# The second block's gates: five steps a layer stand inside runs of small products

## The chip, the core and the metric

The kernel runs on one core of a Trainium2 chip. The metric is the device time of one execution in microseconds, as the median of several runs. The engines are TensorE (PE for its products, PEld for its weight loads), VectorE (DVE), ScalarE (ACT), GpSimd (POOL) and SyncE (SP, which issues most of the DMAs).

## The reference, cut to what matters

Two blocks of different architecture run over 256 tokens of width 1024, each with two layers, all in float32. The first block (gated mixing, attention, cross attention, experts) isn't touched. A layer of the second block computes:

```python
p = n @ w_in                                    # columns for the recurrence, for latent attention, and the gates
p_r, p_k, p_v, p_w, p_a, p_g = split(token_shift(p_rw))
gate_a, gate_b = split(p[..., SHIFT_COLS + MLA_COLS:], 2)      # 2 x 1024 columns
y_a = _rwkv7_time_mix(p_r, p_k, ...) @ w_out_rwkv              # the recurrence
y_b = _mla(q_lat, kv_lat, k_pe, ...) @ w_out_mla               # attention over latents
merged = sigmoid(gate_a) * y_a + sigmoid(gate_b) * y_b
h = h + merged @ w_out
h = h + _conv_ffn(rmsnorm(h), w_ffn_up, conv_w, conv_b, w_ffn_down)
```

The recurrence is, per head of 64 columns (8 heads) and per token, `state = state * w + (state @ a) b + v k`, `y = state @ r`.

## The kernel before

**The recurrence in chunks.** `tensor_rwkv` (TensorE), `vector_rwkv` and `scalar_rwkv` work on the 256 tokens in 8 chunks of 32 (`CH`, `NCH`), for 4 pairs of heads (`PAIRS`) and 2 tiles of 128 tokens (`NT`), so 16 units (`UNITS`). The products inside a chunk are small, 32x32 to 64x64. `chunks` makes, in 64 products, one 32x32 matrix per unit and chunk (L2220); `blocks` multiplies such matrices to invert a triangle (L2238); `wide` makes 128x128 ones (L2230); `turn` transposes (L2210). Then come the rows u (L2314), W and U (L2325), the outputs (L2334), the inner products for the chunks' ends (L2345, first for G, 48 products, then for H, 112), and last the states, one chunk after the other (L2386, L2390), each of which waits for VectorE (L3156). A float32 product is issued as two products and two weight loads, so 64 of the program's are 128 products and 128 loads in the trace.

**The gates between them.** The 2048 gate columns are 4 quarters j of 512, for 2 token tiles t, with 8 slices k of the inner width 1024: 64 steps. A step is one slice of one output tile [128 tokens x 512]. For j = 0 and 1 it is one float32 product (L2191), for j = 2 and 3 it is `exact`: three products of split high and low parts (L578), each with its weight load. These steps depend on nothing in the recurrence; they fill TensorE while ScalarE and VectorE work on the small products' results. `fill(point)` issues the steps of one point of the table `GATE_FILLS`; the order of the steps is fixed (`gate_step`), the table only says how many stand at which point. The points behind step 44 were before:

- "close", steps 45 to 47: ahead of `chunks(4, kt, a0)`, the keys' run of L2220
- "rows", 48 to 52: behind it and eight transposes, ahead of the u products (L2314)
- "wu", 53 to 55: ahead of L2325; "q", 56 and 57: ahead of the outputs; "g", 58: behind the G products
- "h", 59 to 62: behind the H products, while VectorE makes H (L3148); "rest", 63: behind the states

The outputs of t = 0 and 1 sit in PSUM banks 6 and 7. When a tile's eighth slice is done, ScalarE takes the sigmoid out of the bank (`gate_rows` in `scalar_rwkv`, L2764), and the next tile's first step of that bank waits for it (`gates_sig`). For j = 3, the tiles' first four slices are steps 48 to 51 and 52 to 55, the last four 56 to 59 and 60 to 63; step 47 ends a tile of j = 2. ScalarE's stream has its `gate_rows` at fixed points, each taking the tiles that the table says are done there (`gates_done`). The first product of step 48 signals that the weights of j = 2 are no longer read (L2199); SyncE waits for that and loads the next 2 MB into this slot of the ring.

**Who issues what.** There is no scheduler: each engine's instructions stand in the order of the code, and every wait is a semaphore's. An own wait instruction (L2174) shows where a product waits for more than one.

Of the kernel before, what the change touches and what calls it, by code (L numbers as in the profile page):

```python
# [47 lines left out]
PAIRS = RW // P  # L48
# [492 lines left out]
def slab(m, slot, k, n):  # L541

    return m.ring[:, slot, 0:k * n].rearrange("p (k n) -> p k n", n=n)
# [1582 lines left out]
def _gate_fills():  # L2126
    at = 0
    for point, n in (("open", 8), ("prep", 5), ("sums", 3), ("masks", 2), ("second", 3), ("second_wide", 3), ("fourth", 3),
                     ("whole", 2), ("fourth_wide", 3), ("eighth", 2), ("keys", 4), ("block", 3), ("block_wide", 2), ("cross", 2),
                     ("close", 3), ("rows", 5), ("wu", 3), ("q", 2), ("g", 1), ("h", 4)):  # L2130
        GATE_FILLS[point] = (at, at + n)
        at += n
    GATE_FILLS["rest"] = (at, 2 * PAIRS * KD)


_gate_fills()
EXACT_GATES = 2


def gate_step(i):  # L2140

    j, r = i // (2 * KD), i % (2 * KD)
    if j < EXACT_GATES:
        return j, r // KD, r % KD
    return j, r // 4 % 2, r // KD * 4 + r % 4
# [7 lines left out]
def gate_rows_split(m):  # L2153

    room = m.ring_lo[:, PLAN2[W_GATES].slot]
    return room[:, 0:SLAB // 2], room[:, SLAB // 2:], m.hT[:, :, :].rearrange("p k n -> p (k n)")
# [10 lines left out]
def tensor_rwkv(m, pe, l, landed, used):  # L2167
# [3 lines left out]
    tiles = [(p, t) for p in range(PAIRS) for t in range(NT)]  # L2171

    def wait(signal, k=None):
        pe.wait_ge(*at(signal, l, k))  # L2174

    def fill(point):

        for i in range(*GATE_FILLS[point]):
            j, t, k = gate_step(i)
            n = 2 * j + t  # L2180
            out, tokens = ps[:, 6 + t, :], slice(t * P, (t + 1) * P)
            if k == 0:
                if n < 2:
                    wait("kk_root")
                else:
                    wait("gates_sig", n - 1)
            if j < EXACT_GATES:
                if k == 0 and t == 0:
                    landed(W_GATES + j)
                w = slab(m, PLAN2[W_GATES + j].slot, KD, BANK)  # L2190
                ins = mm(out, m.hT[:, k, tokens], w[:, k, :], start=k == 0, stop=k == KD - 1)  # L2191
            else:
                if k % 4 == 0 and t == 0:
                    wait("gate_lo", 2 * (j - EXACT_GATES) + k // 4 + 2)
                rows = [a.rearrange("p (k n) -> p k n", n=T)[:, k, tokens] for a in gate_rows_split(m)[:2]]
                w = [a.rearrange("p (k n) -> p k n", n=BANK)[:, k % 4, :] for a in gate_half(m, j, k // 4)[:2]]
                first, ins = exact(m, out, rows, w, k == 0, k == KD - 1)
                if j == PAIRS - 1 and k == 0 and t == 0:
                    first.then_inc(used(W_GATES + j - 1), 1)  # L2199
            if k == KD - 1:  # L2200
                ins.then_inc(s("gates_full"), 1)
            elif j == EXACT_GATES and t == 1 and k == 3:
                ins.then_inc(s("gates_half"), 1)
# [6 lines left out]
                ins = nc.tensor.transpose(ps[:, b, c0:c0 + P], src[:, 2 * half + i, t * P:(t + 1) * P], m.ident)  # L2210
        ins.then_inc(s("tok_T"), 1)

    def chunks(b, lhs, rhs):

        for i, (p, t) in enumerate(tiles):
            for c in range(CT):
                tokens = slice(t * P + c * CH, t * P + (c + 1) * CH)
                for h in range(2):
                    r = slice(h * HD, (h + 1) * HD)
                    ins = mm(ps[c * CH:(c + 1) * CH, b + h, i * CH:(i + 1) * CH], lhs[r, p, tokens], rhs[r, p, tokens],  # L2220
                             start=True, stop=True)
        ins.then_inc(s("prod_full"), 1)
# [18 lines left out]
    def unit(p, t, h):  # L2241
        return h * PAIRS * NT + p * NT + t

    a0, bt, kt, rr = m.KK, m.A, m.LW, m.C
# [56 lines left out]
    blocks(2, M["D"], M["D2T"])  # L2301
    fill("close")
    wait("prod_masked", 8)
    chunks(4, kt, a0)
    for half in range(2):
        turn((0, 3)[half], a0, half)
    fill("rows")
    wait("prod_masked", 9)
    wait("tok_a", 2)
    for h in range(2):  # L2310
        for i, (p, t) in enumerate(tiles):
            for c in range(CT):
                r = slice(c * CH, (c + 1) * CH)
                ins = mm(ps[r, 4 + h, i * HD:(i + 1) * HD], M["Aak"][r, unit(p, t, h), :],  # L2314
                         m.vtok[r, p, t * P + h * HD:t * P + (h + 1) * HD], start=True, stop=True)
        ins.then_inc(s("u_full"), 1)
# [30 lines left out]
    def head(a, p, t, h):  # L2347
        return a[:, p, t * P + h * HD:t * P + (h + 1) * HD]
# [11 lines left out]
        outputs(g, lambda p, t, h: head(m.vtok, p, t, h), m.Ark, lambda p, t: False, False)  # L2360
    wait("g_set")
    for p, t in tiles:
        for part in range(2):
            for c in range(CT):
                if t * CT + c < NCH - 1:
                    for h in range(2):
                        u1 = m.WU[:, unit(p, t, h), HD:]
                        lhs, rhs = ((head(m.btok, p, t, h), u1), (head(m.ktok, p, t, h), head(m.vtok, p, t, h)))[part]
                        ins = inner(p, t, c, h, lhs, rhs, part == 0, part == 1)
# [984 lines left out]
```

## Time and profile before

| | us |
|---|---|
| median of 3 runs | 2261.44 |
| lowest, highest | 2258.86, 2265.96 |
| the profiled execution | 2257.99 |
| its span, first to last instruction | 2256.2 |
| mean granted TensorE clock | 0.930 of full speed |

The times of single instructions come from the profiled execution. The second block begins at about 1330 us; its layers' recurrences with the gates lie at 1407 to 1517 us and at 1857 to 1966 us. In the rows, "issue" in the chain of waits is time in which TensorE had no instruction under way and waited for nothing that the profile shows. L578 is the line of `exact`, L2345 that of the inner products for G and H.

### The profile page before, as it was taken

The page shows a single profiled execution, that of the slowest core. Times are in us where ns is not written, and L with a number is a line of the kernel's source. Part 1 is how long each engine was busy: PE and PEld are TensorE (multiplying, and loading weights), DVE is VectorE, ACT ScalarE, POOL GpSimd, SP SyncE. Part 2 cuts the span into 40 slices and gives each one's busy share as a digit, 9 for nine tenths or more (in the row PEclk, how much of TensorE's full clock was granted, in tenths as well). Part 3 has the DMA queues.
Part 4 walks back from the last instruction along what each step waited for, and adds up shares of the span by engine and source line. Part 5 has one row for each costly group of instructions (what it writes and reads, how often), then busy time and mean ns, then how long its engine had stood idle before and what let it go on. Part 6 is the DMA issues. An engine that isn't in the chain of part 4 may idle for free.

```text
span 2256.2 us, 38410 instructions
## 1 busy us (share of the span) xinstructions
PE 2035.7 (90%) x17052; PEld 1392.2 (62%) x17052; DVE 894.9 (40%) x1280; ACT 718.2 (32%) x1015; POOL 40.8 (2%) x65
## 2 busy tenths in 40 slices
PE   8999988887779999987787789999999999999998
PEld 6887433333327887432333339675899796758996
DVE  6444211100106444111111117546677475476774
ACT  5444111111105453111111125314444453144442
POOL 1000000000001000000000000000000000000000
PEclk9999888888889998888888889999999999999999
DMA  8246899999996257899999996023754360237540
GB/s 324 85 141 274 365 428 428 428 428 429 429 423 249 75 187 308 360 428 428 429 429 428 428 412 238 4 71 119 235 187 169 107 227 4 76 113 226 187 178 19
DMA packets 139667, 592.33 MB, mean 263 GB/s; under 512 B 5744, under 2 KB 59200, under 8 KB 114448
## 3 DMA queue, kind: packets, MB, share of 16 engines
q1 hardware_dynamic: 138432, 586.67, 65.5%
q0 software_dynamic: 1104, 3.70, 0.4%
q8 instruction: 109, 1.79, 0.3%
q14 instruction: 22, 0.18, 0.0%
HBM read 589.30 MB, written 1.05 MB: 262 GB/s over the span
## 4 chain that ended last, share of the span: by engine, by line
PE 69%; DMA 24%; DVE 3%; ACT 2%; issue 2%; SPq 1%; DVEq 0%; POOLq 0%; ACTq 0%; POOL 0%
PE ps L578 36%; DMA ring<-in_w_up 22%; PE ps L1182 11%; PE ps L2191 3%; PE ps L2006 2%; PE ps L904 2%; DMA ring<-in_w_in 1%; PE ps L1144 1%; PE ps L2238 1%; PE ps L1205 1%; PE ps L1214 1%; PE ps L595 1%; PE ps L1003 1%; PE ps L1099 1%; PE ps L1079 1%
## 5 line engine op out<-in xcount | busy, mean ns | idle before, releaser
L1182 PE MATMUL ps<-ring,area 128*32 128x512 f32 x1920 | 308.5, 716 | 122.1 <-DMA ring<-in_w_up 122.1
L554 DVE TENSOR_TENSOR ring_lo<-ring,slab_hi 128x2048 fp32r<-128x2048 f32 x136 | 311.3, 2291 | 226.7 <-ACT slab_hi L549 226.4
L549 ACT ACTIVATE slab_hi<-ring 128x2048 fp32r<-128x2048 f32 x136 | 260.0, 1913 | 288.1 <-PE ps L578 266.9
L1182 PEld LDWEIGHTS ps<-ring,area 128*32 128x32 f32 x1920 | 72.6, 128 | 312.6 <-issue 159.4
L578 PE MATMUL ps<-hT_hi,slab_hi 128*128 128x256 f32 x832 | 234.7, 282 | 3.0 <-DVE hT_lo L571 1.6
L578 PE MATMUL ps<-hT_lo,slab_hi 128*128 128x256 f32 x832 | 233.4, 280 | 0.0
L578 PE MATMUL ps<-hT_hi,ring_lo 128*128 128x256 f32 x832 | 232.5, 279 | 0.0
L1771 DVE TENSOR_TENSOR area<-ps,par 128x256 f32<-128x256 f32 x32 | 13.6, 425 | 484.9 <-PE ps L1144 484.9
L1421 ACT ACTIVATE area<-ps 128x512 f32<-128x512 f32 x32 | 19.1, 597 | 539.8 <-PE ps L1182 539.8
L1205 PE MATMUL ps<-ring,area 128*32 128x512 f32 x992 | 158.6, 795 | 32.3 <-DVE area L1791 29.8
L578 PEld LDWEIGHTS ps<-hT_hi,slab_hi 128*128 128x128 f32 x832 | 156.0, 188 | 4.2 <-issue 2.2
L578 PEld LDWEIGHTS ps<-hT_hi,ring_lo 128*128 128x128 f32 x832 | 158.0, 190 | 0.0
L578 PEld LDWEIGHTS ps<-hT_lo,slab_hi 128*128 128x128 f32 x832 | 156.3, 188 | 0.0
L1144 PEld LDWEIGHTS ps<-area,xn 128*128 128x128 f32 x1024 | 124.4, 202 | 27.1 <-issue 27.1
L578 PE MATMUL ps<-slab_hi,hT_hi 128*128 128x512 f32 (+1 forms) x320 | 125.2, 391 | 6.1 <-DVE hT_lo L571 4.1
L1144 PE MATMUL ps<-area,xn 128*128 128x32 f32 x1024 | 128.0, 286 | 1.8 <-DVE area L1755 1.8
L578 PE MATMUL ps<-ring_lo,hT_hi 128*128 128x512 f32 (+1 forms) x320 | 123.9, 387 | 0.0
L578 PE MATMUL ps<-slab_hi,hT_lo 128*128 128x512 f32 (+1 forms) x320 | 122.9, 384 | 0.0
L1214 PE MATMUL ps<-area 128*128 128x512 f32 x256 | 118.4, 605 | 0.0
L1205 PEld LDWEIGHTS ps<-ring,area 128*32 128x32 f32 x992 | 36.3, 140 | 131.6 <-issue 90.3
L1214 PEld LDWEIGHTS ps<-area 128*128 128x128 f32 x256 | 46.0, 189 | 73.0 <-issue 45.9
L1793 DVE COPY area<-ps 128x512 f32<-128x512 f32 x32 | 22.1, 691 | 168.6 <-PE ps L1205 168.6
(384 smaller groups left out, 3159.0 us busy)
## 6 DMA issues: line engine op xcount, KB each, us to landing
ring<-in_w_up SPq DMA_DIRECT2D x62, 2048.0 KB, 20.4
ring<-in_w_down SPq DMA_DIRECT2D x62, 2048.0 KB, 21.6
ring<-in_w_gate SPq DMA_DIRECT2D x56, 2048.0 KB, 15.2
ring<-in_w_ffn_up SPq DMA_DIRECT2D x44, 1024.0 KB, 7.7
ring<-in_w_in SPq DMA_DIRECT2D x18, 2048.0 KB, 10.1
ring<-in_w_ffn_down SPq DMA_DIRECT2D x10, 2048.0 KB, 7.8
ring<-in_xattn_w_kv SPq DMA_DIRECT2D x8, 2048.0 KB, 16.8
area<-in_w_gate SPq DMA_DIRECT2D x6, 2048.0 KB, 13.9
```

The source lines that it names most:

```text
L549: return m.nc.scalar.activation(hi, whole, ACT.Copy)
L554: return m.nc.vector.tensor_tensor(lo, whole, hi, ALU.subtract)
L578: ins = m.nc.tensor.matmul(out, lhs[a], rhs[b], start=start and i == 0, stop=stop and i == 2)
L595: ins = m.nc.tensor.transpose(m.ps[:, b, k * T + t * P:k * T + (t + 1) * P], src[:, t, cols(2 * b + k)], m.ident)
L904: ins = mm(out, w[:, k, c * P:(c + 1) * P], rhs[:, k, :], start=k == 0, stop=k == KD - 1)
L1003: ins = mm(ps[:, score_bank(t), h * HD:(h + 1) * HD], m.pT[:, j, kt, :], m.raw[:, kt, c:c + HD], start=kt == 0, stop=kt == 1)
L1144: ins = mm(ps[:, 2, k * CAP:(k + 1) * CAP], m.xn[:, t, k * P:(k + 1) * P], m.onehot[:, t, :], start=t == 0, stop=t == NT - 1)
L1182: ins = mm(ps[32 * g:32 * g + CAP, 1, :], m.tokT[:, k, :], gate_up[i][:, k % 4, (g % 2) * BANK:(g % 2 + 1) * BANK], start=k == 0, stop=k = ...
L1205: ins = mm(ps[32 * c:32 * c + CAP, 2 + nh, :], m.hid[:, c, half, :], down[half][:, c, nh * BANK:(nh + 1) * BANK], start=half == 0, stop=ha ...
L1214: ins = mm(ps[:, 4 + 2 * nh + t, :], m.pick[:, t * P:(t + 1) * P], m.dn[:, nh, :], start=False, stop=True, skip_group_check=True)
L2006: ins = mm(ps[:, 4 * j + i, :], src[:, k, t * P:(t + 1) * P], w[:, k, nh * BANK:(nh + 1) * BANK], start=k == 0, stop=k == 3)
L2191: ins = mm(out, m.hT[:, k, tokens], w[:, k, :], start=k == 0, stop=k == KD - 1)
```

## The change

The table has three new points, and `fill` is called in the midst of three runs of small products: "keys_in" after half of the keys' run, "u_in" between the two halves of the u products, "h_in" between the pairs 0, 1 and the pairs 2, 3 of the H products. The steps keep their order, so the counts of the points between shift: "close" has 45 and 46, "keys_in" 47, "rows" 48 to 50, "u_in" 51 and 52, "wu" 53 and 54, "q" 55 and 56, "g" 57, "h_in" 58 and 59, "h" 60 to 63, and "rest" none.

```diff
@@ -2127,7 +2127,7 @@
-                     ("close", 3), ("rows", 5), ("wu", 3), ("q", 2), ("g", 1), ("h", 4)):
+                     ("close", 2), ("keys_in", 1), ("rows", 3), ("u_in", 2), ("wu", 2), ("q", 2), ("g", 1), ("h_in", 2), ("h", 4)):
@@ -2210,9 +2210,11 @@
-    def chunks(b, lhs, rhs):
+    def chunks(b, lhs, rhs, within=None):
 
         for i, (p, t) in enumerate(tiles):
+            if within and i == len(tiles) // 2:
+                fill(within)
@@ -2301,13 +2303,15 @@
-    chunks(4, kt, a0)
+    chunks(4, kt, a0, "keys_in")
@@ -2301,13 +2303,15 @@
     for h in range(2):
+        if h:
+            fill("u_in")
         for i, (p, t) in enumerate(tiles):
@@ -2360,6 +2364,8 @@
     wait("g_set")
     for p, t in tiles:
+        if p == PAIRS // 2 and t == 0:
+            fill("h_in")
         for part in range(2):
```

The order of TensorE's instructions around the keys' run and the u products, before; ps is PSUM, ring_lo the low parts of the weights, area the recurrence's matrices, x3 of L578 are one step:

```order
L578 MATMUL ps<-ring_lo 128x512 x9
L2220 MATMUL ps<-area 32x32 [waits prod_masked]
L2220 MATMUL ps<-area 32x32 x63
L2210 MATMUL ps<-con,area 128x128 x8
L578 MATMUL ps<-ring_lo 128x512 [waits gate_lo,gates_sig]
L578 MATMUL ps<-ring_lo 128x512 x11
L578 MATMUL ps<-ring_lo 128x512 [waits gates_sig]
L578 MATMUL ps<-ring_lo 128x512 x2
L2314 MATMUL ps<-area,ring 32x64 [waits tok_a,prod_masked]
L2314 MATMUL ps<-area,ring 32x64 x63
L578 MATMUL ps<-ring_lo 128x512 x9
```

And now (the lines have moved by two and four):

```order
L578 MATMUL ps<-ring_lo 128x512 x6
L2222 MATMUL ps<-area 32x32 [waits prod_masked]
L2222 MATMUL ps<-area 32x32 x31
L578 MATMUL ps<-ring_lo 128x512 x3
L2222 MATMUL ps<-area 32x32 x32
L2210 MATMUL ps<-con,area 128x128 x8
L578 MATMUL ps<-ring_lo 128x512 [waits gate_lo,gates_sig]
L578 MATMUL ps<-ring_lo 128x512 x8
L2318 MATMUL ps<-area,ring 32x64 [waits tok_a,prod_masked]
L2318 MATMUL ps<-area,ring 32x64 x31
L578 MATMUL ps<-ring_lo 128x512 x3
L578 MATMUL ps<-ring_lo 128x512 [waits gates_sig]
```

One step has moved from ahead of the keys' run into it, and two from ahead of the u products into them; the wait of step 52 for ScalarE's sigmoid now stands within the u products.

In the H products on TensorE, the place between pair 1 and pair 2 now reads as follows; before, no L578 stood between the rows of L2345:

```order
L2349 MATMUL ps<-xn,area 64x64 x6
L2349 MATMUL ps<-area 64x64 x6
L578 MATMUL ps<-gate_hi,ring_lo 128x512
L578 MATMUL ps<-ring_lo 128x512
L578 MATMUL ps<-gate_hi,ring_lo 128x512 x2
L578 MATMUL ps<-ring_lo 128x512
L578 MATMUL ps<-gate_hi,ring_lo 128x512
L2349 MATMUL ps<-xn,area 64x64 x8
L2349 MATMUL ps<-area 64x64 x8
```

Two steps, 58 and 59, stand behind 56 of the 112 H products. On ScalarE one sigmoid of the gates (L2764, now L2770), that of the tile which step 47 ends, has moved from ahead of the four copies of the turned keys to behind them, as its stream shows now:

```order
L549 ACTIVATE gate_hi<-ring 128x2048 [waits gates_half]
L2770 ACTIVATE ring<-ps,stat 128x512 [waits gates_full]
L2816 ACTIVATE area<-ps 128x4x64 [waits tok_T]
L2816 ACTIVATE area<-ps 128x4x64
L2816 ACTIVATE area<-ps 128x4x64 [waits tok_T]
L2816 ACTIVATE area<-ps 128x4x64
L2770 ACTIVATE ring<-ps,stat 128x512 [waits gates_full]
L2821 ACTIVATE area<-ps 128x8x64 [waits u_full] x2
```

Before, both sigmoids stood ahead of the copies (L2764 x2). VectorE's, GpSimd's and SyncE's instructions keep their order.

## Rows read from the trace of the kernel before

**Rows 1.** Page, parts 1 and 4: busy time of TensorE; the chain by engine

```profile
PE 2035.7 (90%) x17052; PEld 1392.2 (62%) x17052; DVE 894.9 (40%) x1280; ACT 718.2 (32%) x1015; POOL 40.8 (2%) x65
...
PE 69%; DMA 24%; DVE 3%; ACT 2%; issue 2%; SPq 1%; DVEq 0%; POOLq 0%; ACTq 0%; POOL 0%
```

**Rows 2.** Chain that ended last, layer 1: start us, us, what

```profile
1455.11 2.78 PE ps L578 x12
...
1470.39 2.27 PE ps L578 x9
1472.66 1.22 PE ps L2220 x78
...
1474.90 3.44 PE ps L578 x15
1478.34 1.90 PE ps L2314 x122
1480.24 2.62 issue
...
1483.16 3.63 PE ps L578 x9
...
1501.79 1.51 issue
...
1504.16 4.54 PE ps L578 x12
```

**Rows 3.** The same chain, layer 2

```profile
1922.82 1.36 PE ps L2220 x81
...
1931.33 1.86 issue
...
1952.20 1.55 issue
```

**Rows 4.** Windows from block border to block border (first row: the columns)

```profile
core 0: us, PE busy (x) PEld busy (x) DVE busy (x) ACT busy (x) POOL busy (x), PEclk, DMA share, GB/s
1469.31:1472.70 3.39, 3.39 (x154) 2.69 (x140) 2.27 (x2) 0.21 (x2) 0.00 (x0) 1.00 0.02 5
...
1476.58:1482.84 6.26, 3.66 (x130) 2.93 (x128) 0.00 (x0) 0.60 (x1) 0.00 (x0) 1.00 0.87 328
1482.84:1503.29 20.45, 18.93 (x511) 15.89 (x511) 6.16 (x12) 1.79 (x3) 0.00 (x0) 0.92 0.02 4
1500.18:1503.29 3.11, 1.61 (x146) 1.47 (x134) 0.00 (x0) 0.00 (x0) 0.00 (x0) 1.00 0.02 5
...
1923.00:1926.86 3.86, 3.14 (x134) 2.76 (x128) 1.25 (x3) 1.76 (x5) 0.00 (x0) 1.00 0.09 15
```

**Rows 5.** Windows of half a microsecond, same columns

```profile
1470.00:1470.50 0.50, 0.50 (x47) 0.46 (x34) 0.07 (x1) 0.00 (x0) 0.00 (x0) 1.00 0.12 33
1476.00:1476.50 0.50, 0.50 (x4) 0.41 (x3) 0.00 (x0) 0.00 (x0) 0.00 (x0) 1.00 1.23 66
...
1500.50:1501.00 0.50, 0.50 (x69) 0.50 (x59) 0.00 (x0) 0.00 (x0) 0.00 (x0) 1.00 0.14 33
1926.50:1927.00 0.50, 0.13 (x1) 0.12 (x1) 0.00 (x0) 0.00 (x0) 0.00 (x0) 1.00 0.61 94
```

**Rows 6.** DMA queues, window 1480.2:1480.3: packets, MB, share of 16 engines

```profile
q8 instruction: 1, 0.02, 63.8%
```

**Rows 7.** Windows that show the granted clock, columns as in rows 4

```profile
1504.50:1507.50 3.00, 3.00 (x8) 2.32 (x8) 2.18 (x4) 0.69 (x1) 0.00 (x0) 0.50 0.00 0
1926.14:1926.87 0.73, 0.00 (x0) 0.00 (x0) 0.00 (x0) 0.00 (x0) 0.00 (x0) 1.00 0.40 56
```

**Rows 8.** VectorE's timeline, layer 1: start us, us, instruction, idle before

```profile
1504.20 2.48 DVE L3148 TENSOR_TENSOR area<-ps,area 128x512 f32<-128x512 f32 x4 [5.46 <-PE ps L2345]
...
1515.34 1.29 DVE L3160 COPY area<-ps 128x512 f32<-128x512 f32 x2
```

**Rows 9.** TensorE's timeline, end of layer 1's states

```profile
1516.49 0.82 PE L2413 MATMUL ps<-con,area 128*128 128x128 f32 x6
```

## The prediction, made before the changed kernel had run

> **What bounds the kernel now.** I read the page first: TensorE's products are busy for 90% of the span, and the chain of work that ended last runs 69% over TensorE [rows 1]. The change touches one stage only, the recurrence of the second block (1407 to 1517 us in layer 1, 1857 to 1966 us in layer 2). There the chain of waits lies almost wholly on TensorE, so what counts is where TensorE stands still and how fast it is clocked. The chain in order of time [rows 2, 3] shows idle pieces called "issue": no engine is waited for. Two of them in layer 1 are long, 2.62 us after 122 of the 128 products of L2314 and 1.51 us in the midst of the 224 products of L2345. Layer 2 has its twins (1.86 and 1.55 us).
>
> What ends them? Count instructions. Between the ends of the two long idles TensorE runs 511 products, 511 weight loads and, by the code, two waits that are instructions of their own: 1024, four times 256 [rows 4] (both ends lie in idle, so no instruction under way is counted, as in the shorter windows). The idles thus stand at borders of blocks of 256 instructions. A packet of the instruction queue has 0.02 MB [rows 6], and one belongs to each block; in half-microsecond slices it shows as 33 GB/s in an otherwise quiet stretch, about a microsecond after TensorE enters the block before (block entered 1469.31, packet 1470.00 to 1470.50; block entered 1500.18, packet 1500.50 to 1501.00 [rows 4, 5]). So I read the idles as TensorE waiting for the code of the next block, which is asked for only when the block before begins. From entering one block to entering the next it then takes at least 3.1 us (3.11 in the L2345 run), 3.4 to 3.9 in other places [rows 4]. A block of small products is worked off in 1.6 us, a block with wide gates' steps in it takes longer than its successor's code. After each long idle the clock falls: 0.50 in 1504.50 to 1507.50 [rows 7], that is 1.2 GHz in place of 2.4, and four gates' steps there take 4.54 us, where four at full clock take 2.78 [rows 2].
>
> **The change part by part.** A step of j = 2 or 3 is three products and three weight loads; at full clock it costs 2.78/4 = 0.70 us, 0.76 behind small products (2.27/3) [rows 2]. The number of steps, products and instructions is the same; only idle, clock and exposed waits can change.
>
> *Two steps (58, 59) inside the L2345 run.* Before, the block from 1500.18 to 1503.29 holds small products only: 1.61 us of work and 1.51 us idle. Now the run begins one step, six instructions, earlier in the block. The block's first 140 instructions are small products, 12 are the two steps, 104 are small: 244 x 6.3 ns + 2 x 0.70 = 2.93 us. The next block's code comes at 3.11 us in layer 1 and 3.17 in layer 2, so 0.2 us of idle stays: gain 1.3 us a layer, 2.6 in all. If this packet came as late as in the 3.86 us block [rows 4], 0.9 us would stay and the gain would be 0.6 a layer.
>
> *The clock behind it.* The steps 60 to 63 follow the run. An idle of 0.73 us (1926.14 to 1926.87) leaves the clock at 1.00, one of 1.51 brings it down [rows 7]. With 0.2 us of idle I expect it to hold, so that the four steps take 2.78 instead of 4.54 us: gain 1.76, and as much in layer 2, whose idle is as long [rows 3]. Is that cover still enough? VectorE needs 2.48 us after the run for L3148 [rows 8], starting 0.1 later; TensorE would be there at 2.78. It just covers, with 0.2 us to spare. Gain 3.5 in all, bounds 0 and 3.5.
>
> *Step 47 inside the keys' run (L2220).* It no longer stands ahead of it, so the block border 36 instructions into that run would be reached 0.70 to 0.76 us earlier. In layer 1 that block was entered at 1472.70, 3.39 us after the one before, without idle [rows 2, 4]. TensorE would now be there at about 1472.0. The block's code, by the shortest and the longest interval seen, is there 3.1 to 3.4 us after 1469.31, so between 1472.4 and 1472.7. I take 1472.6, since the packet's slice is the ordinary one: 0.6 us of new idle, and what follows on this path was without idle, so it is lost. Bounds 0.4 and 0.7. In layer 2 the same border already waits a little (the run takes 1.36 us where layer 1 takes 1.22 [rows 2, 3]) and the block after it ends in 0.73 us of idle [rows 7], which swallows the step: nothing lost up to there.
>
> *The load that step 48 releases.* The first product of step 48 frees a slot of the ring, and a 2 MB load starts. In layer 1 step 48 starts at 1474.90, the load's first packets come in 1476.00 to 1476.50, and the code packet of the block entered at 1476.58 only between 1480.2 and 1480.3, some 4 us after the load's start instead of 1 us after the block's [rows 2, 4 to 6]; hence the 2.62 us. Steps 51 and 52, now inside the L2314 run, stand on the same side of this border as before (both still ahead of its last products), so this idle stays. In layer 2 step 47 puts step 48 and the load 0.7 us later, while the block is entered at 1926.87 as before. If the packet stays bound to the load's start it comes 0.6 us later; if it is bound to its own request nothing moves. I take the middle, 0.3 us lost.
>
> *Step 55 behind the "wu" point, step 57 behind "q":* they only pass work on from one gap to the next. The waits they covered stay covered: the wait of L2314 for the masked product has 1.0 us of turns and three steps of 0.70 over 1.5 us of VectorE, and L2325's wait for ScalarE's copy (0.60 us) has two steps, 1.4 us. Nothing, 0.4 us gain at most, since two instead of three steps stand in the slow stretch after L2314.
>
> *Step 63 leaves the end.* It stood between the last state product and L2413, which therefore started at 1516.49 [rows 9]; without it L2413 starts 0.75 earlier, at 1515.74, and its 0.82 us, overlapped by its successor's start, are through between 1516.4 and 1516.56. L2406 behind it needs VectorE's copies (1515.34 and 1.29 us, so 1516.63 [rows 8]). That is 0.1 to 0.25 us of new wait a layer; I take 0.25, so 0.5 in all. ScalarE's gate row moved behind its copies has over a microsecond before step 52 needs its bank.
>
> **Sum.** Gains 2.6 + 3.5 = 6.1 us; losses 0.6 + 0.3 + 0.5 = 1.4 us; net 4.7 us. The profiled execution took 2257.99 us (span 2256.2), so 2253.3 for it; the median of the three runs shown is 2261.44, 3.4 above it, and on that base I forecast 2256.7. That is 0.21%, inside the 0.3% (6.8 us) that a measurement of this kernel can tell from no change.
>
> What follows the stage is TensorE's own work (L578) and passes the gain on.
>
> A rule speaks against all this. The Trainium skill, page "Runtime: NRT & Kernel Launch", section "Instruction fetch mechanics", calls the cost of crossing a 16 KiB border of code mostly hidden and gives TensorE 128 KiB, 2048 instructions. By that the L2345 run (448 instructions) could never run dry, and the sum would be that of rival C below. The 2.62, 1.51 and 1.55 us at multiples of 256 speak against the rule here.
>
> **The rivals.** *A, the code packet gets ahead of the load in layer 2.* The load starts 0.7 us later against a block entered as before: first load packets at about 1927.2 instead of in 1926.50 to 1927.00 [rows 5], the code packet due at 1926.87 + 1.0 = 1927.9. Before it lost by more than a microsecond, now by about 0.6. If it wins, the 1.86 us of idle go [rows 3], with them the slow stretch behind (three steps take 3.63 us in layer 1 [rows 2] instead of 2.1, so 1.5) and the 0.3 us above: 3.7 more, 2253.0.
>
> *B, the idle goes but the clock falls all the same,* because small products themselves, not the idle, bring it down. For it: small products fill much of that stretch. Against it: the block of 1469.31, largely 32x32 products and three steps, holds 1.00 [rows 4]. Price 3.5: 2260.2.
>
> *C, the idle is not the lack of code* and goes with the number of small products or is passed to the next border. Then neither idle nor clock improve, and the 0.5 us at the end stay: 2261.9.
>
> *D, slower.* The new idle of 0.6 us in the midst of the keys' run, between products of 32x32, is enough to bring the clock down there too, in both layers, each time 1.75 us, and it still falls behind L2345. The point from which it decides lies between 0.73 us (held) and 1.51 (fell), in a stretch with fewer wide products. 2260.2 + 3.5 = 2263.7.
>
> **How the numbers follow.** Forecast 0.52, A 0.17, B 0.14, C 0.11, D 0.04, the rest 0.02 for waits that I don't see. Faster by over 0.3% means under 2254.7: most of A (0.15) and a third of the forecast, whose terms are uncertain by 1.5 us and whose comparison by another 1.5: 0.32. Slower by over 0.3% means above 2268.2: 0.02. Within: 0.66. The range takes in A with its scatter and goes up past B and C: 2250.5 to 2262.5.
>
> **What would show it.** In the profile after: inside L2345 (now L2349) the idle "issue" piece of 1.5 us is down to 0.2; the four steps before the states take 2.8 us and the clock is 1.00 there; a new piece of about 0.6 us inside the keys' run of layer 1; the 2.6 us piece late in the u products (L2318) is still there in layer 1; a short wait ahead of L2406. The forecast is wrong if an idle still stands at the L2345 border, if the clock is 0.50 in the four steps, or if the state products then wait for VectorE.

## The result, and the profile after

The changed kernel takes 2248.37 us (median of 13 runs, 2243.12 to 2257.01); beside it on the same chip the kernel before took 2258.94 us (median of 13). The ratio is 0.9949, with a 95% interval of 0.9936 to 0.9962: faster by 8.6 to 14.5 us. I had forecast 2256.7, a gain of 4.7 us on a base of 2261.44, and a range down to 2250.5. The time lies below the range. Some 2.5 us of the miss are the base, the rest is the gain.

The profiled execution took 2247.39 us (span 2245.6). The page, part 1 and part 4, as in [rows 1]:

```profile
PE 2025.5 (90%) x17052; PEld 1382.8 (62%) x17052; DVE 894.7 (40%) x1280; ACT 718.1 (32%) x1015; POOL 40.7 (2%) x65
...
PE 68%; DMA 24%; DVE 3%; ACT 2%; issue 1%; SPq 1%; DVEq 0%; POOLq 0%; ACTq 0%; POOL 0%
```

The same 17052 products are busy 10.2 us less, at a mean granted clock of 0.936 where it was 0.930. In the two stages the trace of before has the clock at 0.50 four times, behind each of the four long idles, and that of after not once. The share of "issue" in the chain falls too. Now the chain in layer 1, which answers to [rows 2] (start us, us, what):

```profile
1468.00 1.60 PE ps L578 x6
...
1469.85 0.58 issue
...
1471.01 0.90 PE ps L578 x3
...
1475.68 1.03 PE ps L2318 x64
1476.71 1.58 PE ps L578 x6
1478.30 1.02 PE ps L2318 x64
...
1493.80 1.39 PE ps L2349 x92
1495.19 1.60 PE ps L578 x6
1496.79 1.39 PE ps L2349 x90
1498.18 2.98 PE ps L578 x12
...
1507.79 1.30 DVE area L3166 x2
...
1509.13 1.98 PE ps L2412 x4
```

No idle is left in the H products (L2349), none in the u products (L2318) either, where 2.62 us had stood, and the four steps behind the H products take 2.98 us where they took 4.54. A new idle of 0.58 us stands in the keys' run. Layer 2, which answers to [rows 3]:

```profile
1912.94 1.60 PE ps L578 x6
...
1914.77 0.83 issue
...
1924.42 1.89 issue
...
1944.91 0.12 issue
...
1945.98 2.99 PE ps L578 x12
...
1956.94 1.98 PE ps L2412 x4
```

Here the u products still stand still, for 1.89 us. The granted clock behind the places (windows, columns as in [rows 4]; the first row is of before, behind the idle of 2.62 us, the others of after):

```profile
1484.00:1487.00 3.00, 3.00 (x15) 1.91 (x17) 0.00 (x0) 0.00 (x0) 0.00 (x0) 0.50 0.03 5
```

```profile
1498.50:1501.00 2.50, 2.50 (x12) 1.82 (x10) 2.20 (x4) 0.00 (x0) 0.00 (x0) 1.00 0.00 0
1926.80:1928.20 1.40, 1.40 (x6) 0.90 (x6) 0.00 (x0) 0.56 (x1) 0.00 (x0) 1.00 0.03 13
```

In both rows of after the clock is 1.00, behind the idle of 1.89 us too.

**The balance.** The chain has no gaps, so it can be cut at the steps ahead of the keys' run and at the start of L2406 (now L2412), which before starts thus, behind step 63:

```profile
1515.76 0.90 PE ps L578 x3
...
1517.31 1.72 PE ps L2406 x4
```

| chain between the cuts, us | before | after |
|---|---|---|
| layer 1 (from 1470.39, now 1468.00) | 46.92 | 41.13 |
| of it "issue" | 4.19 | 0.64 |
| of it gates' steps (L578) | 17.26 | 14.81 |
| layer 2 (from 1920.56, now 1912.94) | 47.25 | 44.00 |
| of it "issue" | 4.18 | 2.90 |
| of it gates' steps | 17.30 | 14.82 |

So the two stages give 5.79 + 3.25 = 9.04 us. Of the 10.6 us between the two spans, 2.39 had arisen before layer 1's cut, in code that the change doesn't touch (1470.39 against 1468.00), and 0.83 are lost again between and behind the stages (0.26 of it in each layer, where the first four products of L2412 take 1.98 us and those of L2406 took 1.72). In a second profile of the changed kernel the part before the cut is no shorter (it reaches the two steps at 1472.24), so those 2.39 us are scatter between executions, no effect of the change.

### The profile page after: what moved, and what is told of

It is laid out like the page before. It is cut to its first block, busy times and chain, and to the rows that moved or that the text cites. A ratio compares the mean times of both kernels' runs of the same rounds, so it can differ in the third digit from the quotient of the medians.

```text
span 2245.6 us, 38410 instructions
## 1 busy us (share of the span) xinstructions
PE 2025.5 (90%) x17052; PEld 1382.8 (62%) x17052; DVE 894.7 (40%) x1280; ACT 718.1 (32%) x1015; POOL 40.7 (2%) x65
## 4 chain that ended last, share of the span: by engine, by line
PE 68%; DMA 24%; DVE 3%; ACT 2%; issue 1%; SPq 1%; DVEq 0%; POOLq 0%; ACTq 0%; POOL 0%
PE ps L578 36%; DMA ring<-in_w_up 23%; PE ps L1182 11%; PE ps L2191 3%; PE ps L2006 2%; PE ps L904 2%; PE ps L2240 1%; PE ps L1205 1%; PE ps L1144 1%; DMA ring<-in_w_in 1%; PE ps L1214 1%; PE ps L595 1%; PE ps L1003 1%; PE ps L1099 1%; PE ps L1079 1%
## 5 line engine op out<-in xcount | busy, mean ns | idle before, releaser
L578 PE MATMUL ps<-hT_hi,slab_hi 128*128 128x256 f32 x832 | 234.7, 282 | 3.0 <-DVE hT_lo L571 1.5
L578 PE MATMUL ps<-hT_lo,slab_hi 128*128 128x256 f32 x832 | 233.4, 280 | 0.0
L578 PE MATMUL ps<-hT_hi,ring_lo 128*128 128x256 f32 x832 | 232.5, 280 | 0.0
L578 PEld LDWEIGHTS ps<-hT_hi,slab_hi 128*128 128x128 f32 x832 | 156.0, 188 | 4.2 <-issue 2.2
L578 PEld LDWEIGHTS ps<-hT_hi,ring_lo 128*128 128x128 f32 x832 | 157.9, 190 | 0.0
L578 PEld LDWEIGHTS ps<-hT_lo,slab_hi 128*128 128x128 f32 x832 | 156.3, 188 | 0.0
L1144 PEld LDWEIGHTS ps<-area,xn 128*128 128x128 f32 x1024 | 119.0, 195 | 27.1 <-issue 27.1
L578 PE MATMUL ps<-slab_hi,hT_hi 128*128 128x512 f32 (+1 forms) x320 | 125.6, 392 | 6.4 <-DVE hT_lo L571 4.5
L1144 PE MATMUL ps<-area,xn 128*128 128x32 f32 x1024 | 122.6, 279 | 1.8 <-DVE area L1755 1.8
L578 PE MATMUL ps<-ring_lo,hT_hi 128*128 128x512 f32 (+1 forms) x320 | 124.1, 388 | 0.0
L578 PE MATMUL ps<-slab_hi,hT_lo 128*128 128x512 f32 (+1 forms) x320 | 123.2, 385 | 0.0
```

The source lines that it names most:

```text
L578: ins = m.nc.tensor.matmul(out, lhs[a], rhs[b], start=start and i == 0, stop=stop and i == 2)
L1144: ins = mm(ps[:, 2, k * CAP:(k + 1) * CAP], m.xn[:, t, k * P:(k + 1) * P], m.onehot[:, t, :], start=t == 0, stop=t == NT - 1)
```

## Why the u products no longer stood still

The stage's clearest surprise is the 2.62 us of layer 1. It had hung on a code packet that came some 4 us behind the load's start [rows 2, 5, 6]. After the change the packets stand so (DMA queues; windows 1474.80:1474.90 and 1923.70:1923.80):

```profile
q8 instruction: 1, 0.02, 59.1%
```

```profile
q8 instruction: 1, 0.02, 60.9%
```

and this is what the load and the block do (windows; the load's first packets show as 106 GB/s, and as 78):

```profile
1470.43:1475.61 5.18, 5.18 (x127) 4.03 (x127) 1.26 (x3) 1.78 (x5) 0.00 (x0) 1.00 0.14 21
1471.40:1471.90 0.50, 0.50 (x14) 0.13 (x18) 0.00 (x0) 0.00 (x0) 0.00 (x0) 1.00 0.11 33
1474.80:1475.30 0.50, 0.50 (x4) 0.38 (x3) 0.00 (x0) 0.20 (x1) 0.00 (x0) 1.00 0.74 106
1917.00:1917.50 0.50, 0.50 (x52) 0.45 (x54) 0.00 (x0) 0.00 (x0) 0.00 (x0) 1.00 0.11 33
1920.00:1920.50 0.50, 0.50 (x3) 0.40 (x3) 0.00 (x0) 0.22 (x1) 0.00 (x0) 1.00 1.08 78
```

TensorE enters a block at 1470.43 and the next one at 1475.61. I had reckoned that this next entry asks for the packet, a microsecond after it. But the packet is there at 1474.85, **ahead** of the entry, and 3.36 us behind the packet before it (1471.49, the 33 GB/s of the second row). TensorE's entry at 1475.61 can't have been what asked for it. In layer 1 it beat the load by 0.06 us (the load's first packet is at 1474.91). In layer 2 the packet before came at 1917.10, so the next was due at about 1920.5, the load started at 1920.14, and the packet came at 1923.72: 3.6 us behind the load's start and 3.2 us late, hence the 1.89 us.

Step 47 is what brought the two together. It now stands behind the block's border, between that block's packet and step 48, which releases the load. So the load starts 3.42 and 3.04 us behind the packet before (layers 1 and 2; 2.91 and 3.44 in the second profile of the changed kernel), where it started 2.45 and 2.42 us behind it; in without_keys_in, where step 47 is back ahead of the border, it is 1.94 and 2.43 us.

That the sequencer of TensorE runs ahead of its products and asks for the code, and that it does so once the code before has arrived, is my reading; shown is only that a packet can follow the one before by 3.4 us while TensorE itself is still 0.76 us from the border (where wide steps fill the blocks, the packets are 5 to 6 us apart). It makes a race, and the experiments test it. "Due" below is the packet before + 3.4 us, the earliest time for it: in the eleven passages where the load came later than the packet, it followed by 3.36 to 3.92 us. The times are starts of packets in the trace of one profiled execution each.

| kernel, layer | due | load starts | packet | idle in u |
|---|---|---|---|---|
| before, 1 | 1477.1 | 1476.19 | 1480.25 | 2.62 |
| before, 2 | 1927.5 | 1926.51 | 1930.68 | 1.86 |
| after, 1 | 1474.9 | 1474.91 | 1474.85 | none |
| after, 2 | 1920.5 | 1920.14 | 1923.72 | 1.89 |
| after, again, 1 | 1479.4 | 1478.95 | 1482.70 | 1.81 |
| after, again, 2 | 1925.8 | 1925.79 | 1927.68 | none |
| keys_in_only, 1 | 1475.1 | 1475.10 | 1479.26 | 2.65 |
| keys_in_only, 2 | 1924.1 | 1923.73 | 1927.69 | 2.75 |
| h_in_only, 1 | 1474.9 | 1473.85 | 1477.80 | 2.38 |
| h_in_only, 2 | 1924.8 | 1923.41 | 1927.83 | 2.12 |
| u_in_only, 1 | 1475.6 | 1474.61 | 1478.70 | 2.25 |
| u_in_only, 2 | 1925.0 | 1923.48 | 1927.70 | 1.49 |
| without_keys_in, 1 | 1473.5 | 1472.04 | 1476.32 | 2.29 |
| without_keys_in, 2 | 1920.7 | 1919.76 | 1923.82 | 2.02 |
| before_load49, 1 | 1473.7 | 1473.56 | 1476.44 | 1.88 |
| before_load49, 2 | 1922.5 | 1922.25 | 1925.85 | 1.85 |
| after_load49, 1 | 1477.9 | 1478.66 | 1477.89 | none |
| after_load49, 2 | 1923.9 | 1924.64 | 1924.41 | none |

Where the packet is due 0.1 us or more after the load's start, it comes 2.9 to 4.4 us behind that start; where it is due 0.7 us ahead, it comes before the load; where the two fall within 0.1 us of each other, it goes either way.

## The experiments

"Stage" is TensorE's time from its 18600th to its 20900th record (products, weight loads and its own wait instructions) and from its 28600th to its 31100th, both layers added; these records stand at about the same places of the program in all kernels with as many instructions. It is of one profiled execution, and holds what luck with the clock that execution had. Before: 128.4 us; after: 120.1.

| kernel | stage | ratio to before (95%) |
|---|---|---|
| after_again | 120.4 | 0.9961 (0.9947 to 0.9974) |
| h_in_only | 122.9 | 0.9965 (0.9951 to 0.9979) |
| keys_in_only | 127.4 | 0.9998 (0.9986 to 1.001) |
| u_in_only | 127.4 | 0.9991 (0.9979 to 1.0002) |
| without_keys_in | 122.5 | 0.998 (0.9967 to 0.9994) |
| before_shift128 | 116.6 | 1.0014 (1.0 to 1.0028) |
| before_load49 | 126.2 | 1.0001 (0.9986 to 1.0016) |
| before_load52 | 120.5 | 0.9971 (0.9955 to 0.9987) |
| h_in_load52 | 120.9 | 0.9953 (0.9936 to 0.997) |
| after_load49 | 118.0 | 0.9967 (0.9952 to 0.9983) |
| h_in_load56 | 116.9 | 0.9967 (0.9955 to 0.9978) |
| h_in_load60 | 119.6 | 0.9981 (0.9967 to 0.9996) |

**after_again**, the changed kernel once more.

> The changed kernel once more, as the measure for its parts. Theory (code blocks): about 0.995 of before; in the trace the new idle of about 0.6 us inside the keys' run (L2222) and at most 0.2 us inside the H products (L2349) are there again in both layers. The 2 to 2.6 us idle late in the u products (L2318) is there in a layer exactly if the code packet for that border starts after the load that step 48 releases. Rival (the gain lies elsewhere, before the second block): the stretch from the first gates' step of layer 1 to the last state product of layer 2 is no shorter than before.

The stage takes 120.4 us, as before, but now the idle in the u products stands in layer 1:

```profile
1483.35 1.81 issue
```

Layer 2 has none. The H products' gain is there both times (0.31 us of idle is left in layer 2, above the 0.2 expected); the u products' gain comes in one layer of two, and not the same one.

**One part of the change alone**, in three kernels. Against the changed kernel's table:

```diff
-("close", 2), ("keys_in", 1), ("rows", 3), ("u_in", 2), ("wu", 2), ("q", 2), ("g", 1), ("h_in", 2), ("h", 4)
+("close", 3), ("keys_in", 0), ("rows", 5), ("u_in", 0), ("wu", 2), ("q", 2), ("g", 1), ("h_in", 2), ("h", 4)   # h_in_only
+("close", 2), ("keys_in", 1), ("rows", 5), ("u_in", 0), ("wu", 3), ("q", 2), ("g", 1), ("h_in", 0), ("h", 4)   # keys_in_only
+("close", 3), ("keys_in", 0), ("rows", 3), ("u_in", 2), ("wu", 3), ("q", 2), ("g", 1), ("h_in", 0), ("h", 4)   # u_in_only
```

> Only the two steps inside the H products (steps 58 and 59), keys' run and u products as before; one step less ahead of L2329. Theory: idle inside the H products falls from 1.5 to 0.1-0.2 us and the clock holds behind it, 3.1 us a layer, 6.2 in all, less 0.3 at the end of the states: ratio 0.9974. The idle late in the u products stays at 1.9 to 2.6 us. Rival 1 (small products alone bring the clock down): 2.6 us in all, 0.9988. Rival 2 (the gain of the change comes from the keys' run alone): 1.000.

> Only step 47 inside the keys' run. Theory: a new idle of 0.6 to 0.8 us in that run in both layers; the border late in the u products gets its code packet earlier against the load that step 48 releases, since a step of 0.7 to 0.9 us now stands between that block's code and step 48. Where the packet starts ahead of the load, the idle of 2.6 (1.9) us and the slow clock behind it go: 4 us less in that layer, ratio 0.9985 for one layer and 0.997 for both. The H products keep their 1.5 us. Rival (the order of packet and load has nothing to do with it, the idle in the u products went by the steps inside them): 1.0005, slower by the new idle.

> Only steps 51 and 52 inside the u products. Theory (block's content and packet against load unchanged): idle late in the u products stays at 1.9 to 2.6 us, H products keep 1.5 us, ratio 1.000. Rival (wide products inside the u products let the code keep up): that idle and the slow clock behind it go, 4 us a layer, ratio 0.9965.

(h_in_only also keeps steps 55, 57 and 63 where the change has them.) The H part alone brings 5.5 us of stage; its chain in layer 1 has the idle in the u products and the four steps at full clock:

```profile
1477.89 2.38 issue
...
1501.38 2.98 PE ps L578 x12
```

Each other part alone brings 1.0 us of stage and nothing that the runs can tell from no change. The u products stand still in both layers of all three kernels: wide steps inside them (u_in_only) don't cure it. The chain of keys_in_only, layer 1:

```profile
1470.06 0.56 issue
...
1479.14 2.65 issue
...
1499.23 1.43 issue
...
1501.53 2.98 PE ps L578 x12
```

Step 47 in the keys' run makes its new idle (0.56 us) and, alone, still loses the race for the u products (2.65), in layer 1 by nothing at all (due 1475.1, load 1475.10). And a second thing is seen here: the idle of 1.43 us in the H products stands as before, yet the four steps behind it take 2.98 us, the full clock. In its layer 2, 1.50 us of idle are followed by 4.33 us for them. An idle of this size does not bring the clock down each time. Nor does a longer one: in the fourteen passages of all kernels with an idle in the u products (1.49 to 2.75 us), the clock fell behind seven and held behind seven.

**without_keys_in**, the changed kernel with step 47 back ahead of the keys' run.

```diff
-("close", 2), ("keys_in", 1),
+("close", 3), ("keys_in", 0),
```

> The changed kernel, but with step 47 back ahead of the keys' run; steps 51, 52, 58, 59 stay inside the small products and 63 ahead of the states. If step 47 matters as I first worked it out, the idle of 0.6 to 0.8 us in the keys' run goes, and the stage gains up to 0.6 us a layer on the 120.1 of the changed kernel, or nothing in layer 2. If instead what step 47 did was to let the code packet get ahead of the load (the load then starts 0.7 us after the block's entry more than before), the u products idle 1.8 to 2.7 us again in both layers: stage at 122 to 124 us, ratio 0.9955 to 0.997. Either way the H products have an idle of under 0.3 us and full clock behind them.

The second theory holds, with a ratio (0.998) a little above its 0.9955 to 0.997; the chain in both layers:

```profile
1468.32 0.27 issue
...
1476.44 2.29 issue
...
1479.16 2.86 PE ps L578 x6
...
1924.40 2.02 issue
...
1926.83 1.59 PE ps L578 x6
```

The keys' idle shrinks (0.27 against 0.58), but the u products wait in both layers, and in layer 1 the clock is low behind it (six products in 2.86 us where 1.59 is the full clock's). The stage is 2.4 us longer than with step 47 inside. The step that by itself only costs is what makes the race a tie, and a tie is luck: the changed kernel won it in one layer of two in both of its profiles, keys_in_only in neither.

**The load moved, nothing else.** The signal that frees the ring's slot for the 2 MB load (L2199) is put on another step:

```diff
-                if j == PAIRS - 1 and k == 0 and t == 0:
+                if j == PAIRS - 1 and k == 1 and t == 0:   # step 49
+                if j == PAIRS - 1 and k == 0 and t == 1:   # step 52
+                if j == PAIRS - 1 and k == 4 and t == 0:   # step 56
+                if j == PAIRS - 1 and k == 4 and t == 1:   # step 60
```

> The kernel before, but the 2 MB load into the freed slot is released by step 49 instead of 48, 0.7 us later. Theory (the code packet is asked for some 0.4 us after the load's start plus 0.8): it still loses, the idle late in the u products stays at 1.9 us or more, ratio 1.000. A theory by which the packet waits a fixed time from its own request gives the same idle of 2.6 us; one by which it waits until a fixed time from the load's start gives 3.3 us.

> The kernel before, the load released by step 52, 2.8 us later than by step 48. Theory: the code packet is ahead of the load, the idle late in the u products (2.6 and 1.9 us) goes in both layers, and where the clock fell behind it, it holds: 4.5 us less, up to 7; the idle of 1.5 us in the H products stays. Ratio 0.998. Rival (the load has no part in it): 1.000, idle unchanged.

The kernel before with the load at step 49 still idles 1.88 us in the u products of layer 1 (due 1473.7, load 1473.56: lost) and 1.85 us in layer 2, so 0.7 us aren't enough there. With it at step 52 it reads in layer 1:

```profile
1478.62 1.92 PE ps L2314 x128
...
1486.00 0.35 issue
...
1498.47 1.83 issue
...
1501.17 2.97 PE ps L578 x12
```

All 128 u products run in 1.92 us without a stop, with no step among them, and those of layer 2 too: moving the load alone takes the idle away. A little comes back in L2325 (0.35 us, and 0.64 in layer 2), where the next packet meets the later load. The idle in the H products is still there, 1.83 us. The stage is 7.9 us shorter than before, partly by luck of the clock: behind 1.83 us, and 2.11 in layer 2, it held.

> Steps 58 and 59 inside the H products (as in the run of these alone), and the load released by step 52; step 47, 51 and 52 as before. Theory: both idles of each layer gone and no new one in the keys' run; stage of both layers together 116 to 118 us where the changed kernel has 120 and the kernel before 128; ratio 0.995 or less, so at least as fast as the changed kernel (0.9955). Rival (the changed kernel's gain beyond the H steps comes from step 47 in the keys' run itself): no faster than the H steps alone, 0.9965.

Both cures together. The u and H products have no idle in either layer, but in layer 1 L2329 waits 1.97 us for the packet that now meets the load, with a low clock behind it. The packet came at 1484.25, 5.7 us behind the load's start. The stage (120.9, for 116 to 118 expected) is therefore no better than after.

> The changed kernel, with the signal for the next 2 MB load moved from the first product of step 48 to that of step 49, so the load starts about 0.75 us later. Measured so far: in the changed kernel's profile the code packet came 0.06 us ahead of the load's start in layer 1 (no idle in the u products) and 3.6 us behind it in layer 2 (idle 1.89 us). Race theory: with the load 0.75 us later the code packet is ahead of it in both layers, the u products have no idle in either, and TensorE's record 18600 to 20900 and 28600 to 31100 (the stage) together take about 118 us where the changed kernel took 120.1 and the kernel before 128.4; ratio to before 0.994 to 0.996. Rival (the packet follows the load's start at a fixed distance): the idle in layer 2 stays at 1.9 to 2.7 us and comes later, the stage is at 120 to 123 us. Second rival: a packet is only as early as TensorE's own entry of the block before allows, then the idle in both layers is 2 us or more and the stage is at 124.

The changed kernel with the load at step 49. Its chain, layer 1, then the second half in layer 2:

```profile
1478.73 1.03 PE ps L2318 x64
1479.76 1.58 PE ps L578 x6
1481.34 1.02 PE ps L2318 x64
...
1927.33 1.03 PE ps L2318 x64
```

No idle in the u products in either layer, and a stage of 118.0 us, as the race has it. The ratio (0.9967) doesn't follow: it is above the 0.994 to 0.996 expected, and no better than that of h_in_only. One place outside the stage shows in the trace: 8 us behind the end of layer 2's, from 1980.5 on, the granted clock is 0.50 for 13.7 us, and the records 31100 to 34000 take 217.2 us where they took 212.1 in the kernel before. after_again (216.7) and before_shift128 (217.2) have such a stretch too, the other eleven profiles don't. In none of these three had the clock fallen in layer 2's stage; whether that is the cause stays open. Two windows of layer 1, a block from border to border and the half microsecond with the packet that follows on it:

```profile
1473.46:1478.66 5.20, 5.20 (x128) 4.04 (x128) 1.42 (x3) 1.79 (x5) 0.00 (x0) 1.00 0.03 6
1477.80:1478.30 0.50, 0.50 (x4) 0.41 (x3) 0.00 (x0) 0.24 (x1) 0.00 (x0) 1.00 0.16 33
```

The packet (1477.89) comes 3.39 us behind the one before (1474.50) and 0.8 us ahead of TensorE's own entry at 1478.66, as in the changed kernel.

> The kernel before with steps 58 and 59 inside the H products and with the load signalled at step 56 (first slice of the last four of tile t = 0) in place of step 48, so that it starts behind the u products and behind the W and U products. Race theory: the load no longer meets the code packets of the u products or of L2325, so no idle in either layer there; a packet may lose to it in the output or G products if one is due within 2.4 us of it, else the stage is at 116 to 119 us (the same with the load at step 52: 120.9, since there a packet behind the load cost 1.97 us and a low clock in layer 1); ratio 0.993 to 0.996. Rival (the load is needed at once, and starting it some 10 us later delays the weights that come behind it in the ring): a new wait for weights behind the stage, over 3 us a layer, ratio above 0.998.

> As the one with the load at step 56, but with the signal at step 60, behind the H products, where mainly wide products and then the states' small ones follow. Race theory: no code packet of the u, W and U or H products meets the load, so the stage loses only what a packet behind the load costs in the states, whose products wait for VectorE anyway: stage 116 to 119 us, ratio 0.992 to 0.995, the best of all. Rival: the load comes too late for the next stage's weights, a wait for DMA of 1 us or more a layer appears behind the states and the ratio is above 0.997.

Both take the kernel before with steps 58 and 59 inside the H products. Neither delays later weights: behind the stages no wait for a DMA stands in either chain. But with the load at step 60 the packet that meets it is one in the states (layer 1, layer 2):

```profile
1510.90 0.98 issue
...
1955.48 1.41 issue
```

I had expected this to hide behind VectorE; it didn't, and the ratio (0.9981) is above the 0.992 to 0.995 expected. At step 56 the stage is the shortest of those that leave the borders where they were, 116.9 us, yet the ratio is 0.9967, above the 0.996 expected. The stages of these two profiles are 11.5 and 8.8 us shorter than before's and the ratios give 7.4 (5.0 to 10.2) and 4.3 us (0.9 to 7.4); taken whole, the two profiled executions were no better than most (2250.09 us against a median of 2246.86, and 2251.26 against 2251.66), and up to layer 1's stage they had taken 3.4 and 2.5 us more than the profiled execution of before. That part scatters by 8 us over the thirteen profiles without added waits (the 18600th record comes at 1465.5 to 1473.5 us), and the intervals of the ratios are 5 to 8 us wide, so a gain of the stage of 1 or 2 us can't be read from a ratio. No version is faster than the changed kernel by more than the intervals.

**before_shift128**, the kernel before with 128 wait instructions ahead of the second block's first products, on a signal that has already been given, so that all borders of TensorE's code behind them move by half a block (the trace shows 128 more wait instructions):

```diff
+    if l == 0:
+        for _ in range(128):
+            first_ready(m, pe, l, 0)
```

> The kernel before, with 128 wait instructions (on semaphores long set) put on TensorE at the start of the second block, where it idles for weights. No instruction of the stage changes its order or its wait; only the borders of the 256-instruction blocks move by 128 instructions. Theory: the idles sit at the borders, so in the H products the idle is no longer behind 167 of the 224 products but behind about 103 of them and shorter (its block now holds a part of the slower outputs), 0.4 us instead of 1.5; the idle behind 122 of the 128 u products is gone, since that border now lies in the W and U products, which take longer than the code's delay. The first stage (from step 45 to the start of latent attention) shrinks from 64 to 58-62 us. Rival (the idles belong to what the products do, or to their number): both idles stay behind the same products, 64 us.

Its chain in layer 1 (the lines are moved by three):

```profile
1460.52 0.61 issue
...
1487.81 1.92 PE ps L2317 x128
...
1493.45 0.62 issue
...
1505.72 2.56 PE ps L2348 x168
```

No step stands inside a run of small products, no product is gone, and yet the u products and the H products run through, in layer 2 as well (for the H products I had expected 0.4 us of idle). The idles stand at other places, the new borders; in layer 2 one of 1.19 us stands among the four steps behind the H products. The 116.6 us of stage (the same records, counted 128 later) aren't a gain of the kernel, since the waits ahead of it cost about as much (11.57 us; ratio 1.0014).

The other traces say the same. Number TensorE's records from the program's start, waits included, and divide by 256. In the fourteen traces the chain behind 1400 us has 116 pieces of "issue" longer than 0.25 us, and each of the 116 ends at a record with the remainder 239 or 240, in before_shift128 too. With this rival C falls: the idles belong to the borders, and not to the number or the kind of the products that run there.

## Why the prediction was wrong, step by step

- **Idle in the H products**: forecast 0.2 us left of 1.5. Measured: none in layer 1 and 0.12 in layer 2, so 1.51 + 1.43 = 2.9 us for a forecast of 2.6. Right, and the reason too: h_in_only has it alone.
- **The clock behind it**: forecast 2.78 in place of 4.54. Measured 2.98 and 2.99, 3.1 us in both layers for 3.5. The size was near, but the certainty was not earned. The forecast took it that an idle of 1.5 us brings the clock down and one of 0.7 doesn't. In the ten passages of kernels without steps in the H products and with the borders as before (before, keys_in_only, u_in_only, before_load49 and before_load52, two layers each) the clock fell seven times, at idles of 1.45 to 1.86 us; it held at 1.43, 1.83 and 2.11. In all sixteen passages of kernels with them it held. So full clock behind the H products came with each of them, but part of the 3.1 us is the luck of the profiled execution of before, in which the clock fell both times.
- **Step 47 in the keys' run**: forecast 0.6 us of new idle in layer 1 and none lost in layer 2. Measured 0.58; and in layer 2 0.83 in place of the 0.73 behind it. Right.
- **The load that step 48 releases**: this is the step that failed. I wrote that the idle in layer 1 "stays" and that layer 2 loses 0.3 us, since I counted the packet from TensorE's own entry into the block (1476.58 before), plus a microsecond. By this rule the packet of layer 1 would now have come at 1476.6, 1.7 us behind the load's start; it came at 1474.85, 0.76 us ahead of the entry itself. What fits the traces is the packet before plus 3.4 us. So counted it was due at 1477.1 before the change, against a load at 1476.19, and moving step 47 behind the border brought due time and load within 0.5 us of each other in both profiles of the changed kernel. In layer 1 this gave 2.62 us of idle and 1.36 of clock (three steps at 3.63 us, where full clock takes 2.27), 4.0 us that the sum didn't have. In layer 2 the idle stayed (1.89), but the clock held behind it: 1.3 us more. The clock is luck, since behind such an idle it fell in half of the passages, and so is the layer: in the second profile the idle is gone from layer 2 and stays in layer 1.
- **Rival A** was this mechanism, with a chance of 0.17, and for layer 2 alone. By its row it should have been a rival for each layer. Two profiles show it, once in layer 1 and once in layer 2.
- **Step 63**: from the start of the states to L2406 it took 8.61 us before, 7.71 without the step's 0.90; after, 1501.15 to 1509.13 is 7.98. So 0.27 us of wait, for 0.25 forecast. Right.
- **What the sum left out**: each step put among small products costs some more. Steps 45 to 47 took 2.27 us as nine products, and now 1.60 + 0.90. In all, layer 1's gates' steps are 2.45 us shorter where the clock alone gives 1.56 + 1.36: 0.5 us lost. In layer 2 it is 0.3.
- **Rivals B, C, D**: B falls with the clock rows above, C with before_shift128 and the count of the records. D put a point between 0.73 and 1.51 us from which an idle brings the clock down; there is none in these runs (it fell behind 1.45 us and held behind 2.65). D's idle of 0.58 and 0.83 us in the keys' run left the clock at full (step 47 behind it takes 0.90 us in both layers).

The rule by which I named rival C, of the Trainium skill's page "Runtime: NRT & Kernel Launch", section "Instruction fetch mechanics" (the crossing of a border of code mostly hidden), fails here: 1.4 to 2.8 us of idle at borders in small products. The same section of the Trainium skill says that an engine's sequencer fetches the next page of code itself while the current one runs. The trace agrees as far as it goes: a packet came 0.76 us ahead of TensorE's entry at the border.

With the forecast's 4.7 us, plus 4.0 + 1.3 from the u products, 0.3 from the H idle and 0.3 not lost in layer 2, less 0.4 of clock and 0.8 for the insertions, the sum is 9.4 us; the chains gave 9.04. Read from the table of the chains alone, 4.8 us are less idle and 4.9 us shorter gates' steps, and the rest of the chain is 0.7 us longer. The medians' 10.6 and the second comparison's 0.9961 (8.8 us) lie on both sides.

## To carry to other kernels

In a stage of small products, count the instructions from one block border to the next and ask whether each block of 256 lasts longer than its successor's code takes to come, here 3.1 to 3.4 us; wide work belongs into the blocks that don't, not ahead of them or behind. A large load that starts just before a code packet is due holds it up by some 3 us (2.7 to 4.2 in the rows of the table with an idle), so look for the load as well as for the count. Moving its signal is an edit of one line: four steps later gained 0.3% by itself, one step later nothing, and at steps 52, 56 and 60 the load met other packets (idles of 0.4 to 2.0 us). When two such events lie within half a microsecond, forecast both ends and not the one that the single profile shows.

## What the runs showed of the hardware

- A code packet came 3.4 us behind the one before also when TensorE was still 0.76 us (after_load49: 0.77) from the border. One that was due in the u products after a 2 MB load had begun came 2.9 to 4.4 us after the load's start, though a packet itself takes 0.9 to 1.6 us.
- In the fourteen traces the 116 pieces of "issue" of over 0.25 us behind 1400 us all end at records 256 instructions (or a multiple) apart, whatever work stands there.
- The granted clock held at 1.00 behind idles of 1.83, 1.89 and 2.11 us, and of 2.65 us in keys_in_only (three steps behind it in 2.29 us), and fell to 0.50 behind others of 1.45 to 1.86. What decides it these runs don't show. It could also fall later: three of the fourteen profiles have 10.2 to 13.7 us at 0.50 behind layer 2's stage.
- 128 waits of TensorE on a signal already given are no small thing: in the trace of before_shift128 they start 0.106 us apart, 13.9 us in all, of which 11.57 stand in the chain as one piece of "issue".
